# The experts' first 64 rows picked out by matrix products from the ranks, in place of a gathered block

## The chip, the cores and the metric

The kernel runs on one core of a Trainium2 chip. The metric is the time of one execution on the device in microseconds (us), the slowest core's; with one core there is only that one. TensorE (PE), VectorE (DVE), ScalarE (ACT) and GpSimd (POOL) each work through a list of instructions of their own and wait for each other by semaphores. SyncE (SP) only issues transfers here.

## The reference, cut to what matters

Two layers. Each has a mixer (dilated attention with a gated part in layer 0, an RWKV recurrence in layer 1) and then a mixture of experts; 512 tokens, 1024 features, float32. The change touches the mixture alone:

```python
def _moe(h, router_w, router_b, w1, w3, w2):
    t = h.reshape(-1, D)                                   # 512 x 1024
    s = jax.nn.sigmoid(t @ router_w)                       # 16 experts in 4 groups
    sel = (s + router_b).reshape(n_tok, 4, 4)
    group_score = jnp.sum(lax.top_k(sel, 2)[0], axis=-1)
    g_idx = jnp.argmax(group_score, axis=-1)
    _, local = lax.top_k(sel[jnp.arange(n_tok), g_idx], 2) # two experts of the best group
    ...                                                    # gates: the two scores over their sum
    for e in range(N_EXPERTS):
        hid = jax.nn.silu(t @ w1[e]) * (t @ w3[e])
        y = y + gates[:, e:e + 1] * (hid @ w2[e])
```

`h` is the normed input, times a scale per feature plus a shift per feature.

## The kernel before, in words

Only the chosen expert of a token is computed. Each layer first **routes**. TensorE makes the logits (L2137 of the kernel before). VectorE works out the two chosen experts of each token and writes the one-hot choice `CHX` (function `route`, semaphore `chosen`). TensorE counts, for each token and expert, how many tokens stand before it (bank `rank`, L2295 and L2298). VectorE makes from that a slot for each token and choice, in blocks of 64 rows (`ROWS`), each block for one expert. It writes the slot as two one-hot matrices, `HOTR` (row in the block, L482) and `HOTI` (number of the block, L485 and L489, semaphore `hot`). TensorE multiplies them (bank `list`, L2307, eight products) and so gets, for each block, which token stands in each row. VectorE writes that as integers to `LI` (L503) and the counts per expert to `CN`; then the semaphore `items` opens the expert stage.

Between these steps TensorE runs `keep_warm(out, n)`: n products of `ident` with `ones`, 512 columns each, whose result nobody reads (L2064).

The **expert stage** is a loop over the blocks, two blocks to a turn, with all engines counting along on semaphores of the layer, `M(name)`:

- POOL copies a column of `LI` to `IDX` (L902) and gathers the 64 rows of the block from `xn_dram`, a copy in memory of the normed tokens `XE`, into `Xg` by an indirect transfer (L912). A row is gathered in halves, so that 128 partitions hold it.
- TensorE turns the block (`turn`, four transposes, L2324), ACT and DVE each write four of its eight chunks of 128 features into `XgT`, with scale and shift (`turned`, L1188 and L1654).
- ACT and DVE copy the block's expert weights from one of four slots (`expert_slots`) into a stage (`stage_up`, `stage_down`, L1172 and L1640, L1179 and L1645). TensorE then makes `up` (L2336, 16 products), `turn_hidden` (L2343) and `down` (L2354), and POOL sends the rows out (L923).
- SP loads the weights of the 16 experts, 3 MB each, by three transfers (L735). Experts 0 to 3 are loaded ahead. Expert 4 waits until both engines have staged the last block of expert 0, and so on.

The first turn stands outside the loop. TensorE goes from the list to a `keep_warm` of five products, then waits for the gather of block 0, turns it, and runs `up(0)`, `turn(1)`, `turn_hidden(0)`, `up(1)`, `turn(0)` and so on. Stage 1 of the up weights shares its memory with `XE`, so that it is filled only when block 0 has been read and `xn_dram` is written (semaphore `rows_out`).

In float32 each product of the program stands in the trace as two MATMUL rows and two weight loads (two passes).

## Time and profile before

| | us |
|---|---|
| median of 3 runs | 1369.6 (1367.29 to 1371.43) |
| the profiled execution, its time | 1365.57 |
| its span in the trace | 1363.9 |
| TensorE busy | 1225.5 (90%) |
| DVE, ACT, POOL busy | 841.9, 477.0, 322.9 |
| mean granted TensorE clock | 0.951 of full speed |

Some 1.7 us of the time lie around the span. The granted clock has two levels in this trace, 1.00 (2.4 GHz) and 0.50 (1.2 GHz); the mean comes from how long each holds.

### The profile page before, as it was taken

What the parts mean: (1) busy time and instruction counts of PE and PEld (TensorE: products, weight loads), DVE (VectorE), ACT (ScalarE), POOL (GpSimd) and SP (SyncE); (2) the same over time, 40 slices, a digit from 0 to 9 for tenths busy, and PEclk for the clock granted to TensorE, in tenths of its full rate; (3) what the DMA queues carried; (4) which work ended last, traced back from release to release, by engine and by line L of the source; (5) the groups of instructions that cost most, each with busy time, mean ns of one, the idle gap of its engine ahead of it and who ended that gap; (6) DMA issues with size and microseconds to landing.
All of it is one profiled execution on the core that took longest, in us unless ns stands there. A gap on an engine that the chain in (4) does not pass through costs nothing.

```text
span 1363.9 us, 24844 instructions
## 1 busy us (share of the span) xinstructions
PE 1225.5 (90%) x9304; PEld 825.2 (61%) x9304; DVE 841.9 (62%) x1644; ACT 477.0 (35%) x974; POOL 322.9 (24%) x384
## 2 busy tenths in 40 slices
PE   2989999999799998699999699999999997899980
PEld 2478867847455453584854478888887555455540
DVE  5577575483566664869335677777774325576664
ACT  4000126203366551201038544444443102556541
POOL 1000009100233333100002433443443000333323
PEclk9899899899899999799999899999999998899995
DMA  9677666482999986311110000000001634599945
GB/s 365 217 247 284 213 233 219 134 304 101 319 378 324 378 287 203 125 62 62 62 62 0 31 3 3 21 3 2 3 2 64 233 106 154 200 383 378 380 132 206
DMA packets 125291, 234.77 MB, mean 172 GB/s; under 512 B 9376, under 2 KB 77168, under 8 KB 125200
## 3 DMA queue, kind: packets, MB, share of 16 engines
q1 hardware_dynamic: 114464, 200.42, 42.3%
q0 software_dynamic: 10560, 33.04, 6.8%
q8 instruction: 62, 1.02, 0.3%
q14 instruction: 29, 0.24, 0.1%
q10 hardware_dynamic: 176, 0.05, 0.0%
HBM read 210.42 MB, written 23.07 MB: 171 GB/s over the span
## 4 chain that ended last, share of the span: by engine, by line
PE 67%; DVE 13%; SPq 9%; DMA 5%; issue 4%; ACT 2%; POOL 1%; DVEq 0%; POOLq 0%; ACTq 0%
PE PS L2191 14%; PE PS L2157 8%; SPq L735 8%; PE PS L2336 7%; PE PS L2112 5%; PE PS L2354 3%; PE PS L2535 2%; PE PS L2085 2%; PE PS L2517 2%; PE PS L2423 2%; PE PS L2486 2%; DMA arena<-in_ada_w 2%; DVE arena L1390 2%; DVE arena L1762 2%; PE PS L2261 1%
## 5 line engine op out<-in xcount | busy, mean ns | idle before, releaser
L2336 PE MATMUL PS<-WR,arena 128*64 128x256 f32 x1536 | 180.0, 388 | 5.9 <-ACT arena L1188 4.5
L2336 PEld LDWEIGHTS PS<-WR,arena 128*64 128x64 f32 x1536 | 109.3, 139 | 61.2 <-ACT arena L1188 7.2
L2191 PE MATMUL PS<-WR,arena 128*128 128x256 f32 x480 | 111.4, 393 | 4.3 <-DVE arena L1837 4.2
L2157 PE MATMUL PS<-WR,arena 128*128 128x512 f32 x256 | 113.6, 600 | 0.0
L1390 DVE SCALAR_TENSOR_TENSOR arena<-arena,cact 128x1024 f32<-128x1024 f32 x77 | 99.4, 1291 | 12.1 <-DMA arena<-in_ada_w 6.0
L2191 PEld LDWEIGHTS PS<-WR,arena 128*128 128x128 f32 x480 | 94.0, 197 | 20.2 <-DVE arena L1837 3.4
L1640 DVE COPY WR<-arena 128x2560 f32 x48 | 71.9, 1498 | 38.5 <-issue 26.0
L2354 PE MATMUL PS<-W,arena 128*64 128x512 f32 x384 | 92.9, 604 | 0.9 <-DVE arena L1666 0.9
L923 POOL DMA_DIRECT2D expert_rows<-arena x92 | 49.7, 540 | 157.6 <-DVE arena L1674 150.8
L1172 ACT COPY WR<-arena 128x1536 f32 x48 | 71.0, 1480 | 44.8 <-issue 26.5
L2112 PE MATMUL PS<-arena,WR 128*128 128x512 f32 x192 | 85.5, 601 | 1.1 <-DVE arena L1477 1.1
L2157 PEld LDWEIGHTS PS<-WR,arena 128*128 128x128 f32 x256 | 48.5, 193 | 57.1 <-issue 57.1
L851 POOL TENSOR_TENSOR LO<-GB,tmp 128x256 f32<-128x256 f32 x80 | 66.5, 856 | 62.6 <-DVE GB L1911 52.4
L864 POOL TENSOR_TENSOR rstd<-ms,mhalf 128x4 f32<-128x4 f32 x4 | 4.1, 1028 | 299.1 <-DVE ms L1407 299.1
L1188 ACT ACTIVATE arena<-PS,MOD 128x64 f32<-128x64 f32 x192 | 62.1, 404 | 26.9 <-PE PS L2324 26.8
L912 POOL DMA_INDIRECT arena<-xn_rows,IDX x48 | 56.4, 1176 | 56.3 <-issue 30.6
L2191 PE MATMUL PS<-arena,WR 128*128 128x256 f32 x288 | 65.0, 386 | 4.9 <-DVE WR L1513 4.9
L2112 PEld LDWEIGHTS PS<-arena,WR 128*128 128x128 f32 x192 | 36.9, 193 | 47.3 <-issue 46.3
L2191 PEld LDWEIGHTS PS<-arena,WR 128*128 128x128 f32 x288 | 55.5, 194 | 14.3 <-DVE WR L1513 5.3
L1654 DVE TENSOR_SCALAR arena<-PS,MOD 128x64 f32<-128x64 f32 x192 | 52.7, 337 | 13.4 <-PE PS L2324 13.4
L2064 PE MATMUL PS<-ones,ident 128*128 128x512 f32 x106 | 55.4, 671 | 3.4 <-DVEq L506 2.5
L1179 ACT COPY W<-arena 128x1024 f32 x48 | 50.9, 1061 | 1.5 <-PE PS L2354 1.5
(382 smaller groups left out, 2231.0 us busy)
## 6 DMA issues: line engine op xcount, KB each, us to landing
arena<-in_moe_w SPq DMA_DIRECT2D x96, 1024.0 KB, 13.1
arena<-in_ada_w SPq DMA_DIRECT2D x82, 512.0 KB, 4.7
WR<-in_rwkv_w_rkv SPq DMA_DIRECT2D x6, 2048.0 KB, 8.0
expert_rows<-arena POOLq DMA_DIRECT2D x92, 128.0 KB, 5.5
WR<-in_mix_w_in SPq DMA_DIRECT2D x5, 2048.0 KB, 10.5
WR<-in_mix_w_out SPq DMA_DIRECT2D x2, 2048.0 KB, 7.9
expert_rows<-arena SPq DMA_DIRECT2D x1, 4096.0 KB, 14.7
xn_rows<-WR SPq DMA_DIRECT2D x2, 2048.0 KB, 7.2
```

The costliest lines, as they stand in the source:

```text
L735: sp.dma_start(slot[:, k * 2048:(k + 1) * 2048].rearrange("p (c f) -> p c f", c=2 if k == 2 else KC), io[name][layer, e].rearrange("(c p) ...
L851: gp.tensor_tensor(v4(LMc[k % 2]), v4(LTc), JM[:, lv, :].unsqueeze(1).unsqueeze(1).to_broadcast([P, 2, 2, HH]), ALU.mult).then_inc(sem("lm ...
L912: gp.indirect_dma_start(Xg[:, n, :], None, halves, bass.IndirectOffsetOnAxis(ap=IDX[:, n:n + 1], axis=0)).then_inc(M(f"xg_in{n}"), 16)
L1172: nc.scalar.copy(up_stage[n][:, UP_DVE:UP], expert_slots[:, bass.ds((e + 3) % SLOTS, 1), UP_DVE:UP]).then_inc(M("staged_a"), 1)
L1188: last = nc.scalar.activation(XgT[:, n, c, :], PS[:, n, at:at + ROWS], ACT.Identity, bias=MOD[:, L, c:c + 1], scale=MOD[:, L, 8 + c:9 + c])
L1390: stt(a, rows, cact[:, c:c + 1], a, ALU.mult, ALU.add).then_inc(sem("ada_step"), 1)
L1640: nc.vector.tensor_copy(up_stage[n][:, 0:UP_DVE], expert_slots[:, bass.ds((e + 3) % SLOTS, 1), 0:UP_DVE]).then_inc(M("staged_v"), 1)
L2112: last = mm(out, WR[:, tile % 2, c, f * P:(f + 1) * P], act_T[:, c, :], start=(c == 0), stop=(c == KC - 1))
L2157: last = mm(out, HT[:, c, b * P:(b + 1) * P], WR[:, (first_tile + half) % 2, c, :], start=(c == 0), stop=(c == KC - 1))
L2191: last = mm(out[:, n * 256:n * 256 + 256], left, right, start=(c == 0), stop=(c == 3))
L2336: last = mm(PS[rows2[h], 2 + n, 0:2 * P].rearrange("p (m f) -> p m f", m=2), XgT[:, n, c, :], w[:, :, c, cols(h)], start=(c == 0), stop=(c ...
L2354: last = mm(PS[rows2[h], 6 + n, :], hidT[:, n, c, :], w[:, c, h, :], start=(c == 0), stop=(c == 1))
```

## The change

Block 0 of each layer is no longer gathered. As soon as the ranks stand, DVE works out which tokens have a slot in block 0, which are tokens of expert 0 alone, and writes it as one-hot `HOT0` (128 partitions, four groups of tokens, 64 rows). TensorE multiplies the normed tokens `XE` with it, which gives block 0 already turned: eight chunks of features by four groups of tokens, 32 products with 64 columns. The first two chunks (8 products) stand ahead of the list's product, the other six (24) behind it. The result goes to banks 6 and 7, from which `turned` reads it. POOL begins with block 1, whose gather is now the first.

The order of some other things moves with it. `stage_up(0)` of both engines and `stage_down(0)` read slot 0 directly and no longer a slot looked up in `CN`; `stage_up(0)` of ACT stands ahead of the wait for `items`. The `keep_warm` of three ahead of the list becomes one, the one of five behind it goes, and in layer 1 alone one of seven comes in ahead of the ranking.

```diff
@@ route, DVE
+            ts(sm[:, 0, 0:NB], CH[:, :, 0], -float(MAX_ITEMS * ROWS), float(MAX_ITEMS * ROWS), ALU.mult, ALU.add)
...
             tt(A[:, 0:64], rank, m1, ALU.mult)
+            tt(sm[:, 1, 0:NB], sm[:, 0, 0:NB], b3(rank)[:, :, 0], ALU.add)
             link(tt(B[:, 0:64], rank, m2, ALU.mult))
+            tt(HOT0, io128[:, 0:ROWS].unsqueeze(1).to_broadcast([P, NB, ROWS]),
+               sm[:, 1, 0:NB].unsqueeze(2).to_broadcast([P, NB, ROWS]), ALU.is_equal).then_inc(M("idx"), 1)
@@ moe, POOL
-                for k in range(4):
+                for k in range(1, 4):
                     gather(k % 2, k, peeled=True)
@@ moe, ACT
+                stage_up(0)
+                act.wait_ge(sem("items"), layer + 1)
+                pairs_of = act.value_load(CN[0:1, 0:1], min_val=NEXP // 2, max_val=MAX_ITEMS // 2)
...
-                stage_up(0, expert(0))
-                turned(0, 1)
+                turned(0, 1, 6)
                 act.wait_ge(sem("rows_out"), 16 * layer + 16)
                 stage_up(1, expert(1))
-                stage_down(0, expert(0))
+                stage_down(0)
@@ moe, TensorE
                 out = open_bank(pe, "rank", layer)
+                if layer:
+                    pe.wait_ge(*free("lbias", layer + 1))
+                    keep_warm(bank("lbias", layer), 7)
                 pe.wait_ge(sem("chosen"), layer + 1)
...
-                keep_warm(bank("lbias", layer), 3)
+                pe.wait_ge(*free("logit", layer + 1))
+                keep_warm(bank("lbias", layer), 1)
+
+                def first_rows(out, chunks, at=0):
+                    for k, c in enumerate(chunks, at):
+                        for b in range(NB):
+                            last = mm(out[:, k * ROWS:(k + 1) * ROWS], XE[:, b, c * P:(c + 1) * P], HOT0[:, b, :],
+                                      start=(b == 0), stop=(b == NB - 1))
+                    return last
+
+                pe.wait_ge(M("idx"), 1)
+                pe.wait_ge(sem("xn"), NB * (2 * layer + 2))
+                first_rows(PS[:, 6, :], TURN_ACT[0:2])
                 pe.wait_ge(sem("hot"), layer + 1)
                 for k in range(8):
                     last = mm(out[:, 0:MAX_ITEMS], HOTR[:, k, :], HOTI[:, k, :], start=(k == 0), stop=(k == 7))
                 last.then_inc(filled["list"], 1)
+                first_rows(PS[:, 6, :], TURN_ACT[2:4], 2)
+                first_rows(PS[:, 7, :], TURN_DVE).then_inc(M("tx_up"), 1)
...
-                keep_warm(PS[:, 5, :], 5)
-                turn(0, 16)
-                pair(lambda d: d, [32, 16], first=True)
+                pair(lambda d: d, [16, 16], first=True)
```

TensorE's list in layer 1 before, from the logits (L2137) over the ranks (`CHX`), the keep-warm products (`ones,ident`) and the list (`PS<-LO`) to the first `up` (`WR,arena`). A row that ends in x3 is three products of the program:

```order
L2137 MATMUL PS<-RWs,arena 128x16 x8
L2295 MATMUL PS<-CHX,upper 128x80
L2298 MATMUL PS<-CHX,ones 128x64
L2298 MATMUL PS<-CHX,ones 128x48
L2298 MATMUL PS<-CHX,ones 128x32
L2298 MATMUL PS<-CHX,ones 128x16
L2064 MATMUL PS<-ones,ident 128x512 x3
L2307 MATMUL PS<-LO 128x32 x8
L2313 TENSOR_LOAD CN
L2313 ISA x2
L2064 MATMUL PS<-ones,ident 128x512 x5
L2324 MATMUL PS<-ident,arena 128x128 x4
```

The same place of the changed kernel; `tmp,WR` is `HOT0` with `XE`:

```order
L2146 MATMUL PS<-RWs,arena 128x16 x8
L2073 MATMUL PS<-ones,ident 128x512 x7
L2307 MATMUL PS<-CHX,upper 128x80
...
L2310 MATMUL PS<-CHX,ones 128x16
L2073 MATMUL PS<-ones,ident 128x512
L2322 MATMUL PS<-tmp,WR 128x64 x8
L2331 MATMUL PS<-LO 128x32 x8
L2322 MATMUL PS<-tmp,WR 128x64 x24
L2339 TENSOR_LOAD CN
L2339 ISA x2
L2362 MATMUL PS<-WR,arena 64x256 x16
```

The four transposes and the keep-warm of five are gone, and 32 products with 64 columns stand on both sides of the list. Layer 0 reads the same, without the keep-warm of seven.

VectorE's list behind the ranks, before; `SLF` holds the slots:

```order
L470 SCALAR_TENSOR_TENSOR LO<-LO,PS 128x64
L473 TENSOR_TENSOR LO<-LO 128x64
L474 TENSOR_TENSOR LO<-LO 128x64
L475 TENSOR_REDUCE SLF<-LO 128x4
L476 TENSOR_REDUCE SLF<-LO 128x4
```

And in the changed kernel:

```order
L473 SCALAR_TENSOR_TENSOR LO<-LO,PS 128x64
L476 TENSOR_TENSOR LO<-LO 128x64
L477 TENSOR_TENSOR sm<-sm,LO 128x4
L478 TENSOR_TENSOR LO<-LO 128x64
L479 TENSOR_TENSOR tmp<-io,sm 128x256
L481 TENSOR_REDUCE SLF<-LO 128x4
L482 TENSOR_REDUCE SLF<-LO 128x4
```

Two instructions stand between the ranks and the slots that were not there.

## Rows read from the trace of the kernel before

**Rows 1.** The page's first line.
```profile
span 1363.9 us, 24844 instructions
```

**Rows 2.** Timeline, layer 0: start, us, engine, line, tiles, count, idle time before.
```profile
342.20 1.81 PE L2298 MATMUL PS<-CHX,ones 128*128 128x64 f32 x8
343.85 4.36 PE L2064 MATMUL PS<-ones,ident 128*128 128x512 f32 x6
345.37 0.23 DVE L473 TENSOR_TENSOR LO<-LO 128x64 f32<-128x64 f32 x1
347.98 0.42 DVE L485 TENSOR_TENSOR LO<-io,RF 128x256 f32<-128x256 f32 x1
348.98 1.97 PE L2307 MATMUL PS<-LO 128*128 128x32 f32 x16 [0.76 <-DVE LO L489]
352.29 4.55 PE L2064 MATMUL PS<-ones,ident 128*128 128x512 f32 x10 [1.34 <-DVEq L506]
353.31 2.40 POOL L912 DMA_INDIRECT arena<-xn_rows,IDX  x1 [0.90 <-POOL IDX L902]
362.25 1.29 ACT L1188 ACTIVATE arena<-PS,MOD 128x64 f32<-128x64 f32 x4 [7.94 <-PE PS L2324]
363.60 5.55 PE L2336 MATMUL PS<-WR,arena 128*64 128x256 f32 x32 [1.39 <-ACT arena L1188]
371.12 3.67 PE L2336 MATMUL PS<-WR,arena 128*64 128x256 f32 x32 [0.88 <-ACT arena L1188]
```

**Rows 3.** Timeline, layer 1, the same columns; SPq is SP's queue.
```profile
1153.16 0.69 PE L2295 MATMUL PS<-CHX,upper 128*128 128x80 f32 x2 [7.26 <-issue]
1155.28 4.83 PE L2064 MATMUL PS<-ones,ident 128*128 128x512 f32 x6
1160.48 1.97 PE L2307 MATMUL PS<-LO 128*128 128x32 f32 x16 [0.37 <-DVE LO L489]
1163.61 7.50 PE L2064 MATMUL PS<-ones,ident 128*128 128x512 f32 x10 [1.16 <-DVEq L506]
1172.93 3.67 PE L2336 MATMUL PS<-WR,arena 128*64 128x256 f32 x32 [1.39 <-ACT arena L1188]
1175.27 15.39 SPq L735 DMA_DIRECT2D arena<-in_moe_w  x6
1178.58 3.67 PE L2336 MATMUL PS<-WR,arena 128*64 128x256 f32 x32 [0.88 <-ACT arena L1188]
```

**Rows 4.** TensorE's timeline, layer 0's attention and the modulation's products ahead of the ranks.
```profile
232.32 1.45 PE L2261 MATMUL PS<-arena,W 128*128 128x64 f32 x12
...
333.96 7.88 PE L2085 MATMUL PS<-ones,arena 128*128 128x1 f32 x48
```

**Rows 5.** Windows: stretch, length, TensorE busy (rows), granted clock, DMA share, GB/s.
```profile
334.00:336.00 2.00, 2.00 (x21) 1.00 1.11 357
338.00:340.00 2.00, 2.00 (x12) 0.50 0.15 57
344.00:346.00 2.00, 2.00 (x4) 0.50 1.02 293
348.00:350.00 2.00, 1.24 (x10) 1.00 1.09 377
1164.00:1166.00 2.00, 2.00 (x3) 0.50 0.01 4
```

**Rows 6.** The chain that ended last: start, us, what.
```profile
232.48 1.29 PE PS L2261 x12
342.41 1.61 PE PS L2298 x8
353.31 7.74 DMA arena<-xn_rows,IDX
1300.38 3.67 PE PS L2336 x32
```

**Rows 7.** One window of the expert loop of layer 1, all engines.
```profile
1180.00:1300.00 120.00, 118.77 (x845) 61.09 (x841) 79.96 (x169) 72.24 (x133) 41.87 (x72) 1.00 1.07 379
```

More of the change, by code:

```diff
@@ L893, in moe @@
                 halves = xn_dram.rearrange("s (h f) -> (s h) f", h=2)
-                gathered = gp.alloc_register(f"gathered{layer}")
+                gathered = [gp.alloc_register(f"gathered{layer}{n}") for n in range(2)]
                 indexed = [gp.alloc_register(f"indexed{layer}{n}") for n in range(2)]
@@ L931, in moe @@
                     gp.reg_mov(scaled[n], 2 * n + 6)
-                gp.reg_mov(gathered, 16)
+                for n in range(2):
+                    gp.reg_mov(gathered[n], 16 * n)
                 rows_sent = [gp.alloc_register(f"rows_sent{layer}{n}") for n in range(2)]
@@ L1167, in moe, with stage_up @@
                 counted = lambda d: step[d]
-                def stage_up(n, e):
-                    act.wait_ge(sem("landed"), e)
-                    nc.scalar.copy(up_stage[n][:, UP_DVE:UP], expert_slots[:, bass.ds((e + 3) % SLOTS, 1), UP_DVE:UP]
-                                   ).then_inc(M("staged_a"), 1)
-                def stage_down(n, e, downs=None):
+                def stage_up(n, e=None):
+                    act.wait_ge(sem("landed"), layer * NEXP + 1 if e is None else e)
+                    slot = expert_slots[:, 0, UP_DVE:UP] if e is None else \
+                        expert_slots[:, bass.ds((e + 3) % SLOTS, 1), UP_DVE:UP]
+                    nc.scalar.copy(up_stage[n][:, UP_DVE:UP], slot).then_inc(M("staged_a"), 1)
@@ L1185, in turned @@
+                def turned(n, turns, bank=0):
                     act.wait_ge(M("tx_up"), turns)
-                    for c in (0, 4, 1, 5):
-                        at = c % 4 * P + c // 4 * ROWS
-                        last = nc.scalar.activation(XgT[:, n, c, :], PS[:, n, at:at + ROWS], ACT.Identity,
+                    for k, c in enumerate(TURN_ACT):
+                        last = nc.scalar.activation(XgT[:, n, c, :], PS[:, bank + n, k * ROWS:(k + 1) * ROWS], ACT.Identity,
                                                     bias=MOD[:, L, c:c + 1], scale=MOD[:, L, 8 + c:9 + c])
@@ L1715, in moe @@
                 nc.vector.engine_nop().then_inc(M("yt"), 4)
-                stage_up(0, expert(0))
-                turned(0, 1)
+                v.wait_ge(sem("rest_out"), 16)
+                stage_up(0)
+                turned(0, 1, 7)
+                pairs_of = v.value_load(CN[0:1, 0:1], min_val=NEXP // 2, max_val=MAX_ITEMS // 2)
                 v.wait_ge(sem("rows_out"), 16 * layer + 16)
@@ L1720, in moe @@
                 v.wait_ge(*free("gate", 2 * (L + 1)))
-                stage_down(0, expert(0))
+                stage_down(0)
                 in_order()
```

60 lines of the change are left out of this document (30 added, 30 removed).

## The prediction

> **What bounds the kernel now.** I read the page first, then the chain that ended last, then the timeline of the two places that the diff touches, then windows of 2 us there for the granted clock. The span is 1363.9 us [rows 1] and the execution took 1365.57, which is 4.0 below the median of 1369.6. All sums below are differences, which I put on the median.
>
> In both layers the expert stage cannot start before block 0 is turned, so the stretch from the ranks to the first `up` is on the path. In layer 0 it runs: ranks from 342.20, slots from 345.37, list 348.98, then a wait for the gather of block 0, which took 7.74 us from 353.31 on [rows 2, 6]. Chunks follow at 362.25, first `up` at 363.60, second at 371.12 [rows 2]. In layer 1: ranks 1153.16, list 1160.48, then not the gather but the keep-warm of five, 7.50 us from 1163.61, sets the turn. First `up` is at 1172.93, second at 1178.58 [rows 3]. The reader is to see how differently the same instructions go: ten passes of the keep-warm took 4.55 us in layer 0 and 7.50 in layer 1, and the first `up` 5.55 and 3.67.
>
> That is the clock. It was 0.50 in 1164 to 1166, and in layer 0 0.50 in 338 to 340 and 344 to 346, 1.00 in 348 to 350 [rows 5]. The forecast hangs on which of the two levels TensorE has while it makes block 0.
>
> Behind the start, TensorE sets the pace of layer 0's loop. In layer 1 TensorE and the weights' transfers are both full: 118.77 of 120 us busy, DMA share 1.07 [rows 7].
>
> **The price of one pass.** The new products have 128 partitions and 64 columns. At full clock twelve such passes in the attention took 1.29 us, 0.107 each [rows 4, 6]. At half clock eight passes of the ranking, with 64 columns or fewer, took 1.61 us, 0.20 each [rows 6]. I take twice the full price, 0.21. Block 0 is 64 passes: 16 ahead of the list, 48 behind it, that is 1.7 and 5.1 us at full clock, 3.4 and 10.1 at half.
>
> **Which clock, layer 0.** Ahead of the ranks stand 48 passes with one column, 7.88 us from 333.96 [rows 4]. In them TensorE was busy without a gap, 2.00 of 2.00, and the clock went from 1.00 to 0.50 all the same [rows 5]. It came back between 346 and 348, behind nothing but keep-warm products, three of them from 343.85 to 348.2 [rows 2, 5]. The change leaves one of these, two passes of about 0.85, till 345.6. Then TensorE waits for `HOT0`, and narrow products follow. I expect the clock to stay at 0.50 till the first `up` is well under way, which in this trace had the clock back only in the course of its 5.55 us (at full clock it is 3.67) [rows 2]. I found no place in this trace where the clock came back during products as narrow as the new ones.
>
> The Trainium skill, "TensorE: Matmul & The Clock Gate", Part 1, says that the gate follows how busy the engine has been of late. Taken at its word, TensorE busy with the new products without a gap would be granted full speed; the first rival below is what would come of that here. The trace differs from it for the one-column passes, which kept TensorE busy 2.00 of 2.00 and ended at 0.50 [rows 5].
>
> **The sum, layer 0.**
> - DVE: the product's 4-element add and `HOT0`, 128x256, stand between L473 and the slots. `HOT0` does what L485 does, 0.42 us [rows 2], and its successor starts before it is through; with the small one I take +0.45 on the chain. `HOT0` is ready at 345.37 + 0.14 + 0.24 + 0.45 = 346.2 or so.
> - First 16 passes at half clock: 346.3 to 349.7. `hot` comes at 348.95 + 0.45 = 349.4, so the list, queued behind them on TensorE, waits 0.3.
> - List, 16 passes: 1.97 at full clock before [rows 2], 3.4 now, till 353.1.
> - The 48 passes: 10.1, till 363.2. `turned` and the start of `up` take 1.4 as before (362.25 to 363.60) [rows 2]: 364.6, **+1.0**.
> - `up(0)`: 5.55 before, 7.3 if all of it is at half clock (twice 3.67) [rows 2]: +0 to +1.8. The gather of block 1, now the first, goes out 2.2 us later than the old first one and lands by 363.3, before `up(0)` ends: nothing.
> - Second `up`: +1.0 to +2.8; I take **+2.0**.
>
> **The sum, layer 1.**
> - The keep-warm of seven is 14 passes of 0.43 to 0.45 at full clock (4.55 for ten [rows 2]), 6.0 to 6.4 us in an idle stretch of 7.26 [rows 3]: hidden. At half clock it would be 12 and hold the ranks up by some 4.7; but TensorE comes from wide products there.
> - It keeps the clock up for the ranks: before 1153.16 to about 1155.5, 2.3 us for ten passes [rows 3], now 1.1. **-1.1.** With DVE's +0.45, `hot` comes at 1159.8 instead of 1160.45.
> - But from its end at 1152 to the list at 1159.8 TensorE does 10 narrow passes, one keep-warm product and 16 passes, some 4 of 8 us. In this trace even 0.37 us of wait and the list's passes, behind 4.83 us of keep-warm, were followed by 0.50: 7.50 for ten passes [rows 3, 5]. So the list is at half clock, 3.4 us, till 1163.2. The 48 passes go till 1173.3, the first `up` is at 1174.7 against 1172.93: **+1.8**.
> - `up(0)` is at half clock as well, 7.3 instead of 3.67: the second `up` +5.4.
> - What of that counts: SP's load of expert 4 went out at 1175.27, behind `stage_down(0)` [rows 3], and comes +1.8. TensorE's lateness is swallowed as far as it had idle time, 1.2 of 120 us [rows 7], so up to +4.2. Fourth-last `up` at 1300.38 [rows 6] should move by 1.8 to 4.2 more than layer 0's shift. I take **+3.5**, near the upper end, since TensorE is the fuller of the two.
>
> **Edits at nothing.** DVE's first added instruction lies in its wait for the ranks. ACT's and DVE's `stage_up(0)` ahead of the list: ACT was idle 7.94 us ahead of the chunks [rows 2]; without that cover it would be 1.5. One gather less shortens POOL's list and lengthens nobody's. No instruction is moved past another on SP's queue.
>
> Sum: +2.0 + 3.5 = **+5.5 us, 1375**. The bounds are +1.0 + 1.8 = +2.8 and +2.8 + 4.2 = +7.0.
>
> **The rivals.**
> - *Full clock throughout, faster.* Layer 0: first part till 348.0, list 349.4 to 351.4, rest till 356.5, first `up` at 357.9 (-5.7) and 3.67 long. It then waits for block 1's gather: 353.8 + 7.74 = 361.5, turn and chunks 2.0: second `up` at 363.5, **-7.6**. Layer 1: list 1159.8 to 1161.8, rest till 1166.9, first `up` 1168.3, **-4.6**, and the loop follows. Sum -12.2: 1357.4. For it: the attention's narrow passes ran for tens of us at full clock, so they can hold it. Against it: in both layers the clock is down when they start, or falls in the gaps. It decides at a price per pass of the 48 of some 0.19 (layer 0) and 0.17 (layer 1), the list at half clock: below that the start comes earlier than before. It is also what the page's rule, named above, comes to. Chance 0.20.
> - *Half in layer 0, full in layer 1.* The keep-warm of seven does what it looks like: +2.0 - 4.6 = -2.6, 1367. For it: the ranks at full clock. Against it: the gaps between them and the list. Chance 0.12.
> - *Same mechanism, mostly swallowed.* Only the lower bounds come through, +2.8: 1372.4, because the clock is back early in the first `up` and the weights set layer 1. Chance 0.17.
> - *The forecast,* +4.1 to +8. Chance 0.48. Worse than that (the seven at half clock, or a weight slot freed late in layer 0 with a longer stall): 0.03.
>
> **How the numbers follow.** What can be told from no change is about 0.3%, 4.1 us. Faster: the first rival and a corner of the second, 0.22. Same: most of the second and the third, 0.27. Slower: 0.51. The range goes from 1359 to 1379: it leaves out half of the first rival and the worst cases, about 0.15 to 0.2. Since both signs hold chances, the likeliest case's own range is 1372 to 1378.
>
> **What the new profile would show.** Right: windows at 0.50 from about 337 till past 364, 48 passes of first rows in about 10 us, the first `up` of layer 0 over 7 us long; in layer 1 the ranks in 1.1 us, 1.00 till about 1153, then 0.50 from 1156 or 1160 on till inside `up(0)`. Wrong: 5 us for the 48 passes, then the gather of block 1 as the wait ahead of `turn(1)` in layer 0. The prediction also fails if narrow products bring the clock back from 0.50, or if layer 1's loop has more room than its 1.2 us.

## The result and the profile after

The changed kernel took 1373.21 us (median of 20 runs, 1369.12 to 1376.26), the kernel before beside it 1367.99 (20 runs, 1364.03 to 1371.43). The ratio is 1.0038 (1.0029 to 1.0046): +5.2 us, where +5.5 was predicted. The profiled execution of the changed kernel took 1374.64 us, with a span of 1373.0 and a mean granted clock of 0.939, against 0.951. Its page begins:

```profile
span 1373.0 us, 25051 instructions
PE 1247.5 (91%) x9410; PEld 850.2 (62%) x9410; DVE 843.8 (61%) x1650; ACT 477.0 (35%) x974; POOL 316.9 (23%) x380
```

TensorE is busy 22 us longer than before (1225.5). The products of block 0 take 27.0 us in the two layers (rows below), most of them at the low clock; keep-warm products and transposes that are gone take some back.

The timeline of layer 0, from the ranks to the second `up` (L2362 is the old L2336), to be held against [rows 2]:

```profile
344.08 1.81 PE L2310 MATMUL PS<-CHX,ones 128*128 128x64 f32 x8
345.72 2.06 PE L2073 MATMUL PS<-ones,ident 128*128 128x512 f32 x2
347.24 0.22 DVE L476 TENSOR_TENSOR LO<-LO 128x64 f32<-128x64 f32 x1
347.71 0.42 DVE L479 TENSOR_TENSOR tmp<-io,sm 128x256 f32<-128x256 f32 x1
348.19 3.67 PE L2322 MATMUL PS<-tmp,WR 128*128 128x64 f32 x16 [0.41 <-DVE tmp L479]
351.66 3.57 PE L2331 MATMUL PS<-LO 128*128 128x32 f32 x16
355.04 10.48 PE L2322 MATMUL PS<-tmp,WR 128*128 128x64 f32 x48
366.90 5.18 PE L2362 MATMUL PS<-WR,arena 128*64 128x256 f32 x32 [1.38 <-ACT arena L1189]
374.04 3.67 PE L2362 MATMUL PS<-WR,arena 128*64 128x256 f32 x32 [0.87 <-ACT arena L1189]
```

The 48 passes behind the list take 10.48 us (10.1 predicted), the list 3.57 (3.4). The ranks' second row starts 1.9 us later than before (342.20), ahead of the stretch that the diff touches; over all the traces of this case it starts between 342.0 and 344.8, and in two kernels that are the kernel before up to there at 343.9 and 344.8. From there to the second `up` it is 30.0 us, against 28.9.

Layer 1, to be held against [rows 3]:

```profile
1152.86 6.25 PE L2073 MATMUL PS<-ones,ident 128*128 128x512 f32 x14
1160.23 0.45 PE L2307 MATMUL PS<-CHX,upper 128*128 128x80 f32 x2 [1.11 <-DVE LO L452]
1160.52 1.00 PE L2310 MATMUL PS<-CHX,ones 128*128 128x64 f32 x8
1163.82 2.36 PE L2322 MATMUL PS<-tmp,WR 128*128 128x64 f32 x16 [1.35 <-DVE tmp L479]
1166.90 3.62 PE L2331 MATMUL PS<-LO 128*128 128x32 f32 x16 [0.71 <-DVE LO L495]
1170.33 10.48 PE L2322 MATMUL PS<-tmp,WR 128*128 128x64 f32 x48
1182.19 5.42 PE L2362 MATMUL PS<-WR,arena 128*64 128x256 f32 x32 [1.38 <-ACT arena L1189]
```

The keep-warm of seven fits into the old idle time with 1.11 us to spare. The ranks' ten passes take 1.3 us (1160.23 to 1161.52) in place of 2.3. The clock falls in the course of the first 16 narrow passes, and the list and the other 48 run at the low one. From the ranks' start to the first `up` it is 22.0 us, against 19.8 (the second `up` is at 1189.58).

Windows of 2 us over the two places (TensorE's busy time and rows, granted clock, DMA share, GB/s):

```profile
358.00:360.00 2.00, 2.00 (x12) 0.50 1.10 349
368.00:370.00 2.00, 2.00 (x14) 0.50 0.04 12
370.00:372.00 2.00, 2.00 (x20) 1.00 0.23 65
1162.00:1164.00 2.00, 0.65 (x4) 1.00 1.02 410
1164.00:1166.00 2.00, 2.00 (x16) 0.82 0.06 21
```

In layer 0 the clock stays at 0.50 for some 30 us, from 340 to 350 with some waits and from 350 to 364 with narrow passes back to back at 2.00 of 2.00 busy, and comes back only inside the first `up`, which is 256 columns wide. The Trainium skill, "TensorE: Matmul & The Clock Gate", Part 1, has the gate follow how busy the engine has been of late. By that rule the 48 passes would have been granted 1.00 and taken 5.1 us; this trace does not agree: it gave them 0.50 and 10.48 us.

The loop of layer 1, for [rows 7]:

```profile
1190.00:1310.00 120.00, 120.00 (x859) 61.77 (x855) 81.99 (x170) 74.32 (x134) 44.52 (x74) 1.00 1.07 378
```

The 1.2 us in which TensorE waited in this window before are gone. The window of [rows 7] ends inside that wait: the step of the loop in which it lies took 8.04 us (1292.34 to 1300.38), all others 6.32, so it was worth 1.7 us.

**Where the two profiled executions part.** They differ by 9.1 us, more than the medians. The same rows in both give this table; the last column is what the stretch itself adds.

| reached | before | after | this stretch adds |
|---|---|---|---|
| counts of the ranks, layer 0 | 342.20 | 344.08 | +1.9, ahead of the change |
| second `up`, layer 0 | 371.12 | 374.04 | +1.0 |
| ranks, layer 1 | 1153.16 | 1160.23 | +4.2, hardly touched |
| second `up`, layer 1 | 1178.58 | 1189.58 | +3.9 (first `up` +2.2) |
| end of the span | 1363.9 | 1373.0 | -1.9 |

The two touched stretches add 4.9 us. The other three rows add 4.2 in sum; the experiments below help to tell whether they belong to the change.

### The profile page after: what moved, and what is told of

Its sections match the earlier page's. It is cut to its first block, busy times and chain, and to the rows that moved or that the text cites. A ratio compares the mean times of both kernels' runs of the same rounds, so it can differ in the third digit from the quotient of the medians.

```text
span 1373.0 us, 25051 instructions
## 1 busy us (share of the span) xinstructions
PE 1247.5 (91%) x9410; PEld 850.2 (62%) x9410; DVE 843.8 (61%) x1650; ACT 477.0 (35%) x974; POOL 316.9 (23%) x380
## 4 chain that ended last, share of the span: by engine, by line
PE 76%; DVE 13%; DMA 4%; issue 2%; ACT 2%; POOL 1%; SPq 1%; DVEq 0%; POOLq 0%; ACTq 0%
PE PS L2200 14%; PE PS L2362 12%; PE PS L2166 8%; PE PS L2380 6%; PE PS L2121 5%; PE PS L2559 2%; PE PS L2541 2%; PE PS L2094 2%; PE PS L2510 2%; PE PS L2447 2%; DMA arena<-in_ada_w 2%; PE PS L2322 2%; PE PS L2350 2%; DVE arena L1398 2%; DVE arena L1771 1%
## 5 line engine op out<-in xcount | busy, mean ns | idle before, releaser
L2362 PE MATMUL PS<-WR,arena 128*64 128x256 f32 x1536 | 181.2, 390 | 5.2 <-ACT arena L1189 4.5
L2362 PEld LDWEIGHTS PS<-WR,arena 128*64 128x64 f32 x1536 | 108.5, 140 | 62.2 <-ACT arena L1189 6.1
L1649 DVE COPY WR<-arena 128x2560 f32 (+1 forms) x48 | 71.9, 1499 | 33.9 <-issue 25.6
L1175 ACT COPY WR<-arena 128x1536 f32 (+1 forms) x48 | 71.0, 1479 | 12.9 <-SPq L748 11.1
L918 POOL DMA_INDIRECT arena<-xn_rows,IDX x46 | 48.8, 1061 | 65.3 <-issue 32.9
L1183 ACT COPY W<-arena 128x1024 f32 (+1 forms) x48 | 51.0, 1063 | 1.5 <-PE PS L2380 1.5
L995 POOL TENSOR_TENSOR arena<-arena 128x512 f32<-128x512 f32 x8 | 10.1, 1264 | 171.1 <-DVE arena L2054 171.1
```

The costliest lines, as they stand in the source:

```text
L1175: nc.scalar.copy(up_stage[n][:, UP_DVE:UP], slot).then_inc(M("staged_a"), 1)
L1183: nc.scalar.copy(down_stage[n][:, DOWN_DVE:2048], slot).then_inc(M("staged_a"), 1)
L1649: nc.vector.tensor_copy(up_stage[n][:, 0:UP_DVE], slot).then_inc(M("staged_v"), 1)
L2362: last = mm(PS[rows2[h], 2 + n, 0:2 * P].rearrange("p (m f) -> p m f", m=2), XgT[:, n, c, :], w[:, :, c, cols(h)], start=(c == 0), stop=(c ...
```

## The experiments

Each ratio is taken against the kernel before, run on the same chip; that took 1367.6 to 1368.4 in each set. Beside the medians I use the two stretches that the change touches, from the counts of the ranks (`CHX,ones`, layer 0) or the first row of the ranks (layer 1) to the second `up`, the stretch between them, and the tail behind the second `up` of layer 1. All in us, from the rows of each profiled execution:

| kernel | median | layer 0 | between | layer 1 | tail |
|---|---|---|---|---|---|
| before | 1367.99 | 28.9 | 782.0 | 25.4 | 185.3 |
| changed | 1373.21 | 30.0 | 786.2 | 29.4 | 183.4 |
| the seven alone | 1368.6 | 29.1 | 786.4 | 24.5 | 184.0 |
| changed, without the seven | 1376.07 | 29.9 | 786.0 | 31.8 | 183.5 |
| all behind the list, warm | 1375.23 | 30.8 | 785.9 | 30.3 | 183.6 |
| all behind the list, cold | 1379.27 | 33.2 | 786.1 | 32.9 | 183.5 |
| narrow with wide between | 1372.14 | 29.3 | 782.8 | 28.8 | 183.8 |
| wide products, half ahead | 1359.4 | 20.7 | 788.4 | 22.2 | 183.4 |
| wide, 3/4 and all ahead | 1357.59 | 21.7 | 788.6 | 19.3 | 183.5 |
| the same without the seven | 1359.42 | 21.3 | 788.0 | 21.4 | 183.5 |
| wide, half and all ahead | 1357.62 | 22.0 | 787.0 | 19.3 | 183.5 |
| before, layer 0 held up | 1376.63 | 35.8 | 786.6 | 25.4 | 183.6 |
| before, layer 1 held up | 1375.48 | 26.6 | 786.1 | 31.4 | 185.4 |

One execution stands behind each row of stretches, and unchanged code does not take the same time in each. Layer 0's stretch is the same code in the kernel before, in the seven alone and in the kernel held up in layer 1: 28.9, 29.1 and 26.6 us. In the last, the first `up` ran at 1.00 and took 3.67 us in place of 5.55. A difference of 1 or 2 us in one stretch of one trace is therefore not shown to be the edit's.

### The keep-warm of seven alone

Put into the kernel before:

```diff
                 out = open_bank(pe, "rank", layer)
+                if layer:
+                    pe.wait_ge(*free("lbias", layer + 1))
+                    keep_warm(bank("lbias", layer), 7)
```

> The kernel before with the keep-warm of seven ahead of layer 1's ranking and nothing else. Theory (the loss is the half clock under the first rows; the seven only speed the ranks by 1.1 us and the clock falls in the gaps behind them): within 2 us of before, most likely 0.5 to 1 us faster. Rival (the seven themselves cost, being queued ahead of the ranks): slower by 1 to 5 us, and this alone would be much of the +5.2.

Measured: 1368.6 us, ratio 1.0001 (0.9989 to 1.0014). Its timeline in layer 1:

```profile
1160.55 2.82 PE L2064 MATMUL PS<-ones,ident 128*128 128x512 f32 x6
1165.74 1.97 PE L2310 MATMUL PS<-LO 128*128 128x32 f32 x16 [2.37 <-DVE LO L489]
1168.87 7.60 PE L2064 MATMUL PS<-ones,ident 128*128 128x512 f32 x10 [1.16 <-DVEq L506]
```

The ranks and the keep-warm of three now run at the full clock (2.82 us for six passes, 4.83 in [rows 3]). That only leaves TensorE idle for 2.37 us ahead of the list, and the clock falls again: ten passes of keep-warm still take 7.60 us (7.50 before). The stretch of layer 1 is 0.9 shorter, less than the medians can tell.

### The change without them

```diff
-                if layer:
-                    pe.wait_ge(*free("lbias", layer + 1))
-                    keep_warm(bank("lbias", layer), 7)
```

> The changed kernel without the keep-warm of seven. Theory: the ranks of layer 1 take 2.3 us again and the first 16 passes are at half clock throughout; 1 to 2 us slower than the changed kernel, so 6 to 7.5 us slower than before. Rival (the seven cost time): faster than the changed kernel by 1 us or more.

Measured: 1376.07, ratio 1.0056 (1.0035 to 1.0077), 2.9 above the changed kernel's median; the two intervals overlap, but the stretch of layer 1 is longer by 2.4 in the traces as well. Its timeline in layer 1:

```profile
1163.48 3.68 PE L2319 MATMUL PS<-tmp,WR 128*128 128x64 f32 x16 [0.41 <-DVE tmp L479]
```

The first 16 passes take 3.68 us in place of 2.36, and the ranks 2.3 in place of 1.3. So in the changed kernel the seven do pay: they keep the clock up for the ranks and half of the first products, though not for the list and what follows.

### All new products behind the list, with and without more keep-warm

If the place ahead of the list costs the clock, it should help to leave the keep-warm ahead of the list as it was or larger, and to make all 32 products behind it. The first kernel:

```diff
-                keep_warm(bank("lbias", layer), 1)
+                keep_warm(bank("lbias", layer), 5 if layer else 3)
...
-                first_rows(PS[:, 6, :], TURN_ACT[0:2])
                 pe.wait_ge(sem("hot"), layer + 1)
...
-                first_rows(PS[:, 6, :], TURN_ACT[2:4], 2)
+                pe.wait_ge(M("idx"), 1)
+                pe.wait_ge(sem("xn"), NB * (2 * layer + 2))
+                first_rows(PS[:, 6, :], TURN_ACT)
                 first_rows(PS[:, 7, :], TURN_DVE).then_inc(M("tx_up"), 1)
```

> The changed kernel with all 32 products behind the list and wide keep-warm products in the gap ahead of it: three in layer 0, five in layer 1, in place of one. Theory (clock): 64 passes of first rows at full clock in both layers, 6.9 us; layer 0's second up about 7 us earlier than before, bound there by the gather of block 1, layer 1's first up 2.8 us earlier: 8 to 10 us faster than before. If narrow products let the clock fall in one of the layers: 0 to 6 us faster. Rival (the products and DVE's additions cost more than the gather, whatever the clock): still 2 us or more slower than before.

Measured: 1375.23, ratio 1.0055 (1.0033 to 1.0077): slower than before by 7.5 us. The theory had it 8 to 10 faster, or up to 6 faster if the clock fell in one layer. The time is the rival's, by which the products and DVE's additions cost more than the gather whatever the clock; but the trace shows them at the low clock, in both layers. Its timeline in layer 0 and windows in both:

```profile
343.62 5.25 PE L2073 MATMUL PS<-ones,ident 128*128 128x512 f32 x6
349.16 1.97 PE L2328 MATMUL PS<-LO 128*128 128x32 f32 x16 [0.28 <-DVE LO L495]
350.96 13.01 PE L2322 MATMUL PS<-tmp,WR 128*128 128x64 f32 x64
```

```profile
350.00:352.00 2.00, 2.00 (x20) 0.99 1.13 369
352.00:354.00 2.00, 2.00 (x12) 0.50 1.00 395
1166.00:1168.00 2.00, 2.00 (x19) 0.93 0.00 0
1168.00:1170.00 2.00, 2.00 (x12) 0.50 0.00 0
```

The keep-warm does bring the clock back, and the list runs at full speed. But about 1 us into the new products it falls to 0.50, with no gap in TensorE's work, and stays there for all the rest: 13.01 us for 64 passes, 0.20 each. Layer 1 does the same behind ten passes of keep-warm. I had put the fall in layer 1 down to the gaps. Here it comes without one: behind 5.25 us of 512-column products, a wait of 0.28 us and the list, whose passes have only 32 columns (1.97 us), the new products do not hold the clock.

The second kernel has the same order and the one keep-warm product of the changed kernel:

```diff
-                first_rows(PS[:, 6, :], TURN_ACT[0:2])
                 pe.wait_ge(sem("hot"), layer + 1)
...
-                first_rows(PS[:, 6, :], TURN_ACT[2:4], 2)
+                first_rows(PS[:, 6, :], TURN_ACT)
```

> The changed kernel with all 32 products behind the list, with one keep-warm product ahead of it as there. Theory: all 64 passes at half clock behind the list, 13.6 us instead of 10.5, so the start comes 3 us later in each layer than in the changed kernel: 4 to 6 us slower than the changed kernel, 9 to 11 slower than before. Rival (the quarter ahead of the list only holds the list up): about as fast as the changed kernel.

Measured: 1379.27, ratio 1.0079 (1.006 to 1.0098), 6 us above the changed kernel. In layer 0 TensorE waits 3.49 us for the slots, and the 64 passes behind the list take 13.89. The quarter of the products ahead of the list is worth something: at the low clock it fills time in which TensorE would wait.

### Wide products between the narrow ones

Keep-warm products of 512 columns between the narrow ones might keep the clock up and, though added work, save time. The edit, on top of the first kernel above:

```diff
-                first_rows(PS[:, 6, :], TURN_ACT)
-                first_rows(PS[:, 7, :], TURN_DVE).then_inc(M("tx_up"), 1)
+                keep_warm(..., 2)
+                first_rows(PS[:, 6, :], TURN_ACT[0:2])
+                keep_warm(..., 1)
+                first_rows(PS[:, 6, :], TURN_ACT[2:4], 2)
+                keep_warm(..., 1)
+                first_rows(PS[:, 7, :], TURN_DVE[0:2])
+                keep_warm(..., 1)
+                first_rows(PS[:, 7, :], TURN_DVE[2:4], 2).then_inc(M("tx_up"), 1)
```

> As the version with all products behind the list and three (layer 0) or five (layer 1) keep-warm products ahead of it, and in addition two keep-warm products (512 columns) behind the list and one after every eight of the narrow products, five in all, 4.3 us of more work a layer at full clock. Theory (clock, not work): the clock stays at 1.00, the 64 narrow passes take 6.9 us instead of 13, and the first up of each layer comes 2 us earlier than in that version in spite of the added work and takes 3.7 instead of 5.1 us: faster than that version by 5 us or more, within 3 us of before on either side. Rival (the clock has no part in it, only the amount of work counts): slower than that version by 6 to 9 us, 14 us slower than before.

Measured: 1385.09, ratio 1.0122 (1.0108 to 1.0137). This time says nothing on the question. I had the keep-warm written to the bank in which block 0 stands, which changed layer 1's routing and gave its loop one more pair of blocks. Only its clock is of use: 1.00 through the narrow products but for the first of them (0.79 and 0.84 in the windows in which they start). The same kernel with the keep-warm written to the drained bank of the ranks:

```diff
-                keep_warm(bank("lbias", layer), 2)
+                pe.wait_ge(*free("rank", layer + 1))
+                keep_warm(bank("rank", layer), 2)
```

> The version with wide products between the narrow ones once more, the keep-warm products now written to the drained bank of the ranks. (In the one before they overwrote the bank in which block 0 stood; the choice of experts of layer 1 changed with it, and with that the number of blocks.) Theory (clock, not work): narrow passes at 0.107 as in that trace, first up of layer 1 within 1 us of the version with everything behind the list in spite of 3.3 to 4.3 us of added work, that up 3.7 instead of 5; overall between that version's time and 4 us less, 1370 to 1376. Rival (only the amount of work counts): 8 us or more slower than that version, 1383 or above.

Measured: 1372.14, ratio 1.0029 (1.0016 to 1.0042). Its timeline and windows in layer 1:

```profile
1164.57 3.07 PE L2073 MATMUL PS<-ones,ident 128*128 128x512 f32 x4
1167.43 2.51 PE L2322 MATMUL PS<-tmp,WR 128*128 128x64 f32 x16
...
1170.69 1.89 PE L2322 MATMUL PS<-tmp,WR 128*128 128x64 f32 x16
...
1179.25 3.67 PE L2368 MATMUL PS<-WR,arena 128*64 128x256 f32 x32 [1.38 <-ACT arena L1189]
```

```profile
1166.00:1168.00 2.00, 2.00 (x6) 0.50 0.00 0
1174.00:1176.00 2.00, 2.00 (x14) 1.00 0.00 0
```

The first sixteen narrow passes take 2.51 us, the other three sixteens 1.89 each, and the first `up` 3.67. The five wide products cost 6.3 us in layer 1, part of it at the low clock, and yet the kernel is 3.1 us faster by the medians than the one without them (1375.23; the intervals just overlap), and its two stretches are 1.5 us shorter each. In this stretch the clock stayed up with 512-column products among the 64-column ones, and fell without them. To hold it this way eats nearly all that it gives.

That is not the same as a rule on width. In the attention, groups of 8 to 16 passes of 64 columns stand between products with 128 to 512 columns, and one group of 32 passes (3.68 us from 248.99 in the trace of before) ran through at 1.00. And in layer 1's recurrence of the changed kernel's own trace, products of another shape, 64 partitions and 64 columns, are all that TensorE does from 786.46 on, and the clock came back during them:

```profile
786.00:788.00 2.00, 1.54 (x28) 0.50 0.00 0
788.00:790.00 2.00, 2.00 (x46) 0.54 0.03 8
790.00:792.00 2.00, 1.99 (x60) 1.00 0.00 0
```

They follow each other much faster (60 rows in 2 us, against 12 rows of the new products in 2 us, at 0.50). Why those bring the clock back and the new products do not is not shown.

### The same block, made with wide products

The products can be turned round. With `HOT0` as the weights and the normed tokens as the moving side, each product has 512 columns, and 8 do the work of 32. It keeps one keep-warm product ahead of the list in layer 0 and two in layer 1. The block then comes out not turned, as the gather would have left it, and one copy by ACT and the four transposes are needed again, and POOL's gather of block 2 waits for the transposes of block 0, as before the change. Of the edit, TensorE's part:

```diff
-                            last = mm(out[:, k * ROWS:(k + 1) * ROWS], XE[:, b, c * P:(c + 1) * P], HOT0[:, b, :],
+                def first_rows(blocks):
+                    for b in blocks:
+                        for h in range(2):
+                            last = mm(PS[rows2[h], 6, :], HOT0[:, b, :], XE[:, b, h * 512:(h + 1) * 512],
...
+                first_rows(range(2))
                 pe.wait_ge(sem("hot"), layer + 1)
...
+                first_rows(range(2, NB)).then_inc(sem("gelu"), 1)
+                pe.wait_ge(sem("gelu"), 2 * layer + 4)
+                for c in range(4):
+                    last = nc.tensor.transpose(PS[:, c // 2 * 4, cols(c % 2)], Xg[:, 0, cols(c)], ident[:, :])
```

> The changed kernel with block 0 made in the other way round: HOT0 is the weight (64 columns, two halves side by side) and the normed tokens are the 512 moving columns, 8 products of the program in place of 32, four ahead of the list and four behind it; ACT copies the block out and TensorE turns it with four transposes as it does the others; keep-warm of two in layer 1 and one in layer 0 behind the ranks. Theory: wide passes bring the clock back and hold it, block 0 is ready some 6 us earlier than in the kernel before in both layers, layer 0 then waits for the gather of block 1: 9 to 13 us faster than before. If only the clock of one layer comes back: 3 to 8 us faster. Rival (making the block on TensorE cannot beat the gather): within 2 us of before or slower.

Measured: 1359.4, ratio 0.9932 (0.9917 to 0.9947): 9 us faster than before. Its timeline in layer 0:

```profile
346.73 2.43 PE L2324 MATMUL PS<-WR,tmp 128*64 128x512 f32 x8 [0.41 <-DVE tmp L479]
351.70 1.94 PE L2324 MATMUL PS<-WR,tmp 128*64 128x512 f32 x8
356.37 3.67 PE L2368 MATMUL PS<-WR,arena 128*64 128x256 f32 x32 [1.38 <-ACT arena L1189]
```

Block 0 costs 4.4 us of products in place of 14.2 (3.67 + 10.48), and the first `up` starts at 356.37, where the changed kernel had 366.90.

Then with more of it ahead of the list, three of the four groups of tokens in layer 0 and all in layer 1:

```diff
-                first_rows(range(2))
+                ahead = 4 if layer else 3
+                last = first_rows(range(ahead))
```

> The version with block 0 from wide products, with more of them ahead of the list: three of four groups of tokens in layer 0, all four in layer 1. Theory: in layer 1 the wide products fill the gap in which the clock fell; the list comes 0.6 us later, but nothing stands between it and the turn, and the first up comes 3 us earlier; layer 0 is bound by the gather of block 1 and moves by less than 0.5 us. 2 to 4 us faster than the version with two and two, 1356. Rival (layer 1's end is set by the weights' transfers alone): same as that version.

Measured: 1357.59, ratio 0.9924 (0.9911 to 0.9936), the fastest of all: 10.0 us below the kernel before beside it. Its timeline in both layers, and the wait that its chain shows in layer 0:

```profile
347.15 3.88 PE L2324 MATMUL PS<-WR,tmp 128*64 128x512 f32 x12 [0.41 <-DVE tmp L479]
356.67 3.67 PE L2372 MATMUL PS<-WR,arena 128*64 128x256 f32 x32 [1.39 <-ACT arena L1189]
362.61 0.75 PE L2360 MATMUL PS<-ident,arena 128*128 128x128 f32 x4 [2.26 <-DMA arena<-xn_rows,IDX]
...
1156.96 3.65 PE L2324 MATMUL PS<-WR,tmp 128*64 128x512 f32 x16 [0.49 <-DVE tmp L479]
1165.53 5.16 PE L2372 MATMUL PS<-WR,arena 128*64 128x256 f32 x32 [2.54 <-DVE arena L1663]
```

```profile
355.78 6.78 DMA arena<-xn_rows,IDX
```

In layer 0 the next wait is the gather of block 1, which the prediction's first rival had named. TensorE waits 2.26 us for it, the clock falls, and the second `up` takes 6.18 in place of 3.67. In layer 1 the first `up` starts 12.2 us behind the ranks, against 22.0 in the changed kernel and 19.8 before. The step from the kernel ahead of it is 1.8 us by the medians and 1.1 by the ratios; the intervals overlap.

This one without the keep-warm of seven:

> The version with wide products ahead of the list, without the keep-warm of seven ahead of layer 1's ranking. Theory: the ranks and the first wide passes of layer 1 are at half clock, so the list comes 2 to 3 us later: 2 to 4 us slower than with the seven. Rival (the seven are worth nothing, as they were on the kernel before): same.

Measured: 1359.42, ratio 0.9935 (0.9923 to 0.9947), 1.8 us above; the intervals overlap, but layer 1's stretch is 2.1 longer. In the two kernels that make block 0 on TensorE the seven are worth some 2 to 3 us.

And this one with two groups of tokens ahead in layer 0, in place of three:

```diff
-                ahead = 4 if layer else 3
+                ahead = 4 if layer else 2
```

> Wide products as before, with two of the four groups of tokens ahead of the list in layer 0 (as in the first wide kernel) and all four ahead of it in layer 1 (as in the second). In the second kernel layer 0 gained nothing at the first up, the gather of block 1 came 1 us later against the ranks, TensorE waited 2.26 us for it, the clock fell in that wait and the second up took 6.18 us in place of 3.67. Theory (the late gather and the fall of the clock cost on the path): this mix starts the third up of layer 0 some 3 us earlier against the ranks than the second kernel did, and is 1 to 3 us faster than its 1357.6. Rival (layer 0's start is given back later, the weights' transfers set it): the same as the second kernel within 1 us.

Measured: 1357.62, ratio 0.9924 (0.9906 to 0.9941), the same as with three. Here the clock was slow in the first `up` of layer 0 and no longer in the second:

```profile
356.90 5.36 PE L2372 MATMUL PS<-WR,arena 128*64 128x256 f32 x32 [1.38 <-ACT arena L1189]
...
370.55 3.67 PE L2372 MATMUL PS<-WR,arena 128*64 128x256 f32 x32
```

The third `up` starts 28.3 us behind the counts of the ranks (342.25), against 30.5 with three groups ahead (343.04 to 373.57). The theory had that right, but the medians are the same, as the rival said; a choice as fine as this one can't be told here.

What the wide kernels gain in layer 0 does not all reach the end. Their stretch between the layers is 787.0 to 788.6 us, against 786.1 to 786.6 in the three other traces of layer 0 as it was before. From the second to the last `up` of layer 0 they take 146.3 to 148.3 us, the kernels that start later 144.0 to 145.0. In the kernel with three groups ahead 2.5 us of that are the second `up` at the low clock. The rest of the difference lies in steps between 450 and 490 us in which ACT and DVE wait for an expert's weights. So an early start of layer 0 is in part given back.

### The kernel before, held up in one layer

Whether a late start of the expert stage is swallowed or grows, and what the untouched 4.2 us are, can be asked of the kernel before. Nine products of keep-warm stand between the gather of block 0 and its turning, in one layer alone:

```diff
+                if not layer:        # layer 0 alone; "if layer:" in the other kernel
+                    pe.wait_ge(M("xg_in0"), 16)
+                    keep_warm(PS[:, 5, :], 9)
                 turn(0, 16)
```

> The kernel before, with a keep-warm of nine products between the landing of block 0's gather and its turning, in layer 0 alone: the first up there 8.0 us later, and 3.67 in place of 5.55 long as the clock is up, so the second up some 6 us later. Theory (what is late at the second up of layer 0 is late by the same amount at the end): 6 us slower than before. Rival (a later start of layer 0 costs more further on, as the 4.2 us of unchanged stretches in the changed kernel's trace would have it): 8 or more slower. Other rival (swallowed in layer 0's loop or mixer): 4 or less.

> The same nine products in layer 1 alone, ahead of the turning of block 0, where the clock is up and both ups take 3.67: first and second up 8.0 us later. Theory (the loop swallows the 1.2 to 1.9 us that TensorE had idle, and no more): 6.1 to 6.8 slower than before. Rival (the loop gives nothing back, or costs more, as the medians of the changed kernel against its traced terms might have it): 8 or more slower. Other rival (more room than that): 5 or less.

Measured for layer 0: 1376.63, ratio 1.0067 (1.005 to 1.0083). Its stretch is 6.9 us longer than before, the time 6.8 to 11.4. For layer 1: 1375.48, ratio 1.0056 (1.0039 to 1.0072); stretch +6.0 and not 8.0, since the keep-warm of five took 4.55 us there in place of 7.50 (the nine 7.99), time +5.3 to +9.8. So in neither layer is a start swallowed that is late as a whole, and if more than 1:1 comes through, the medians (+8.6 and +7.5) can't show it for sure. I had expected 1.2 to 1.9 us of room in layer 1.

This does not test the room that the prediction spoke of. There, TensorE was to be late against the transfers, since the first `up` is slow while the load of expert 4 goes out in spite of it. The nine products hold up both alike. The load of expert 4 starts at 1175.27 before [rows 3], and in the kernel held up in layer 1 and the changed one at:

```profile
1185.59 120.90 SPq L735 DMA_DIRECT2D arena<-in_moe_w  x36
```

```profile
1184.84 118.50 SPq L741 DMA_DIRECT2D arena<-in_moe_w  x36
```

From there to the second `up` it is 3.31 us before, 3.31 in the kernel held up in layer 1 (1188.90), and 4.74 in the changed one (1189.58). The tail goes with that distance. Before and held up in layer 1 it holds one step longer than 6.32 us, 8.04 (from 1292.34) and 8.12 (from 1302.66), where ACT and DVE wait for an expert's weights. The rows are of before, before, and held up in layer 1:

```profile
1296.34 1.47 ACT L1172 COPY WR<-arena 128x1536 f32 x1 [4.73 <-SPq L742]
1300.38 3.67 PE L2336 MATMUL PS<-WR,arena 128*64 128x256 f32 x32 [0.67 <-DVE arena L1654]
```

```profile
1310.78 3.67 PE L2336 MATMUL PS<-WR,arena 128*64 128x256 f32 x32 [0.67 <-DVE arena L1654]
```

Over all the traces but that of the 1385.09 kernel, whose loop is longer, it is this:

| load of expert 4 to the second `up` | traces | steps over 6.32 us, in sum | tail |
|---|---|---|---|
| 3.31 | before; held up in layer 1 | 1.7; 1.8 | 185.3; 185.4 |
| 3.31 | the seven alone | 0.4 | 184.0 |
| 2.99 | narrow with wide between | 0.4 | 183.8 |
| 4.35 to 5.86 | the nine others | none | 183.4 to 183.6 |

The kernel held up in layer 0 is among the nine: its layer 1 is the code of before, its first `up` there ran at the low clock, and it had no stall. These traces fit the prediction's account: what TensorE is late against the load is swallowed as far as there was a stall, 0.4 us in some executions and 1.7 or 1.8 in others. It is not shown by a kernel of its own, in which TensorE alone is late, and what makes the stall long or short no run separates. From the start of the ranks to the end, the changed kernel's layer 1 takes 212.8 us. The same stretch with layer 1 as before took 210.7 in the trace of before and 209.0 in that held up in layer 0. The change adds 2.0 or 3.8 us there, depending on which one it is held against.

The stretch between the layers is the other oddity. Three kernels whose layer 0 is that of before, but for the nine products in one of them (the seven alone, and the two here), show 786.1 to 786.6, as the changed kernel does with 786.2. The 782.0 of the profiled execution of before is what is odd. Of the 4.2 us, 2.5 stand at one place of layer 1's recurrence, where TensorE has waited 7.7 us and restarts at the low clock. In the trace of before the clock was back at 777, and it is 25.2 us from there (772.66) to the next group's first transpose. In the changed kernel's (777.51) it was back at 790, and it is 27.7, and in all twelve other traces 27.5 to 28.1. The code is the same.

## Why the prediction was right, and where it was off

- **The clock.** Right in both layers: 0.50 from 340 on until the first `up` of layer 0; in layer 1 the ranks in 1.3 us, then the fall. I had placed the fall there at the list, because of the gaps. It came inside the first 16 narrow products (0.82 in that window), and the kernel with everything behind the list shows that it comes without a gap too.
- **List and narrow passes.** Predicted 3.4 and 10.1, measured 3.57 and 10.48 in layer 0. A pass costs 0.218 us, a little over the 0.21 taken from the attention's rows. The first `up` started 0.4 later than predicted in each layer (+1.4 and +2.2, where +1.0 and +1.8 stood in the sum); these passes are most of it.
- **DVE's added work.** Predicted +0.45 on the chain. From the product's first row to the last write of the slots it was 3.06 us (L473 at 345.37 to L489 at 348.43) and is 3.48 (L476 at 347.24 to L495 at 350.72): +0.42, in both layers. The first products start at 348.19, right behind `HOT0` (347.71 + 0.42).
- **The first `up`, over-sized.** The sum took its length as +1.0 in layer 0 and +3.6 in layer 1, up to all of it at the low clock (7.3 us). It took 5.18 and 5.42, that is -0.4 and +1.7, since the clock came back in its course. The predicted sign "over 7 us long" did not come. So layer 0 gave +1.0 at the second `up` (predicted +2.0, its lower bound), and layer 1 +3.9, where +5.4 was predicted. The +1.0 is less than the spread of that stretch in unchanged code.
- **The keep-warm of seven.** Hidden, with the ranks faster by 1.0, where 1.1 was predicted. Alone it is worth nothing that can be measured, and some 2 to 3 us in the changed kernel.
- **The loop of layer 1.** I predicted that what is late against the weights is swallowed as far as TensorE had idle time, 1.2 us, and took +3.5 of 5.4. The idle time of [rows 7] was a stall on an expert's weights, worth 1.7 us in full, and in the changed kernel's trace it is gone: at the end +2.0 of the +3.9 are left against the trace of before. That fits the kind of thing predicted, which no kernel tests by itself. The size is not settled, since other executions have a stall of only 0.4 at the same distance from the load.
- **The sum.** Measured terms: +1.0 in layer 0 and +2.0 to +3.8 in layer 1, so +3.0 to +4.8 us. The medians say +5.2 (4.0 to 6.3 by the ratio's interval). That the predicted +5.5 lies so near is in part luck: the first `up` was over-sized by 1.4 and 1.9, and against that stand 0.4 in each layer and what is left between the terms and the medians, 0.4 to 2.2 us, for which no run shows a cause.

The profiled pair differs by 9.1, as the one execution of before was 2.4 us below its median and had the short stretch between the layers, 2.5 us of it by the clock in the recurrence. **What stays open** is why the clock returns early there in one execution, the other 1.7 us of that stretch, its 782.8 in the kernel with wide between, and the size of layer 1's stall.

**The rivals.** Full clock throughout is ruled out by the windows. Half in layer 0 and full in layer 1 as well, and the kernel made to give it just that (keep-warm ahead, all behind the list) lost the clock too. Mostly swallowed was right in that the clock came back early in the first `up`; with it +3.0 us of traced terms are as near to this rival's +2.8 as the medians are to the forecast. The medians speak for the forecast: their interval begins at 4.0.

The first rival rested on the attention's narrow passes, read as holding the clock for tens of us. They do not stand alone there, as shown above, so they were no measure for 48 in a row. What the rival said would follow a fast block 0 did follow in a kernel with other work in its place. With 512-column products the second `up` comes 7.2 us earlier in layer 0 and 6.1 in layer 1 than before (7.6 and 4.6 by the rival), the gather of block 1 is what layer 0 waits for, and the kernel is 10.0 us faster than before, where the rival gave 12.2. Part of the difference is what layer 0's loop gives back.

## What to carry to other kernels

Price a new block of products at the clock that it will itself bring about, not at that of its neighbours: 64-column products cost 0.11 us a pass in one place and 0.22 in another. Where the operands of a product can be swapped so that the long side moves, try that before adding work that keeps the clock up. Here the swap gave 14 to 16 us over the changed kernel. In a loop that also waits for transfers, ask of a late engine what it is late against: a start that is late together with the transfers loses all of it (held up by 6.0 us, 5.3 to 9.8 us slower), one that is late against them can use up a stall. And before a difference of 1 or 2 us between two profiles is given to an edit, look how far the same code differs between executions: here by 2.5 us in one stretch.

## What the runs showed of the chip that I had not expected

- 64-column products lost the full clock about 1 us after a list at full speed (1.97 us with 32 columns), in spite of 5.25 us of 512-column work ahead of the list and with TensorE busy 2.00 of 2.00. In the attention's stretch the same shape ran at 0.107 us a pass [rows 4], in groups of up to 16 between wider products and once 32 in a row. Which of the differences counts was not tried.
- 64-column products on 64 partitions, in the recurrence, had the clock back from 0.50 at 790 us in the changed kernel's trace.
- Five 512-column products among them in each layer made the kernel some 3 us faster, and three quarters of the narrow passes took 0.118 us each (1.89 for sixteen) in place of 0.20 (13.01 for 64).
- A keep-warm whose effect is plain in its own rows (the ranks 1.3 us in place of 2.3) was worth nothing where a wait followed it, and 2 to 3 us where work did.
- The same code of layer 1 stalled once for 1.7 us on an expert's weights when the second `up` came 3.31 us behind the load (a step of 8.04 in place of 6.32), and not when it came 4.99 behind.
- Behind the same 7.7 us wait of the recurrence the clock came back 5 us after TensorE restarted in one execution and 12 us in another (772.66 to 777, 777.51 to 790); the same code took 25.2 us in the first and 27.5 to 28.1 in the thirteen others.
